# Four row blocks of the mixed activations split inside the sample's latent loop, and the rotary score products of two sequences issued as a pair

## The reference, cut to what matters

```
q = (rmsnorm(cq) @ w_q_up)                      # 8 MLA heads: 64 plain + 32 rotary columns each
s = (q_nope . k_nope + q_pe . k_pe) * MLA_SCALE # keys from the latent cache ckv, rotary keys kpe
o_mla = softmax(s) @ v
mixed = concat([o_mla (512), ret_y (256), o_sb (256)])
x = x + mixed @ w_out                           # 1024 x 1024
x = x + memory_attend(x); x = x + conv_ffn(x)
```

## Time and profile before

| | us |
|---|---|
| median of 3 runs | 1745.48 (1745.2 to 1748.55) |
| the profiled execution | 1748.12 |
| its span | 1746.3 |
| PE busy | 1703.1 (98%) |
| DVE busy | 1076.1 (62%) |
| ACT busy | 537.6 (31%) |
| POOL busy | 493.6 (28%) |
| granted clock of TensorE, mean | 0.996 |

### The profile page before, as it was taken

How to read it: one execution, slowest core, us unless ns; L and a number is a source line. 1 busy time by engine, 2 the same in 40 slices (tenths; PEclk the granted TensorE clock), 3 DMA queues, 4 the chain that set the end, 5 groups by cost and what they waited for, 6 DMA issues and landing times.

```text
span 1746.3 us, 26437 instructions
## 1 busy us (share of the span) xinstructions
PE 1703.1 (98%) x10471; PEld 1562.2 (89%) x10471; DVE 1076.1 (62%) x1439; ACT 537.6 (31%) x955; POOL 493.6 (28%) x219
## 2 busy tenths in 40 slices
PE   7999999999999989999999999999999999999997
PEld 7998899776666669998899999999999999999996
DVE  6864466786656644536487566565655656566567
ACT  6311121486655541114243220202112121121234
POOL 1772122000000103431044343333333424243331
PEclk9999999999999999999999999999999999999999
DMA  5222111411122303415311111111111111111113
GB/s 213 85 76 77 52 38 37 133 36 61 62 94 67 112 28 108 150 53 216 119 49 37 49 37 48 36 48 36 48 36 48 36 48 36 48 36 48 37 46 109
DMA packets 35005, 119.28 MB, mean 68 GB/s; under 512 B 4976, under 2 KB 8016, under 8 KB 32496
## 3 DMA queue, kind: packets, MB, share of 16 engines
q1 hardware_dynamic: 32624, 108.76, 19.2%
q10 hardware_dynamic: 2304, 9.44, 1.6%
HBM read 100.73 MB, written 15.17 MB: 66 GB/s over the span
## 4 chain that ended last, share of the span: by engine, by line
PE 93%; DVE 3%; ACT 2%; issue 1%; POOL 0%; DMA 0%; ACTq 0%; DVEq 0%; SPq 0%
PE scores L1931 35%; PE bank L1931 33%; PE scores L2159 3%; PE bank L2213 3%; PE bank L2237 2%; PE scores L2004 2%; PE bank L2263 2%; PE scores L1953 1%; PE scores L2179 1%; PE bank L1940 1%; PE scores L2337 1%; PE scores L2336 1%; DVE y_sumsq L1894 1%; PE bank L2230 1%; PE bank L2477 1%
## 5 line engine op out<-in xcount | busy, mean ns | idle before, releaser
L854 POOL TENSOR_TENSOR w_hi<-w_raw,zero 128x1024 fp32r<-128x1024 f32 x96 | 188.5, 1964 | 1179.9 <-PE bank L1931 477.6
L1931 PE MATMUL scores<-act_hi,w_hi 128*128 128x384 f32 x960 | 324.2, 338 | 0.0
L1931 PE MATMUL scores<-act_hi,w_lo 128*128 128x384 f32 x960 | 322.6, 336 | 0.0
L1931 PE MATMUL scores<-act_lo,w_hi 128*128 128x384 f32 x960 | 322.5, 336 | 0.0
L857 POOL TENSOR_TENSOR w_lo<-w_raw,w_hi 128x1024 fp32r<-128x1024 f32 x96 | 251.5, 2619 | 7.5
L1859 DVE TENSOR_TENSOR x<-bank,x 128x384 f32<-128x384 f32 x216 | 120.4, 558 | 103.6 <-PE bank L1931 103.6
L1931 PEld LDWEIGHTS scores<-act_hi,w_hi 128*128 128x128 f32 x960 | 180.5, 188 | 0.6 <-issue 0.2
L1931 PEld LDWEIGHTS scores<-act_lo,w_hi 128*128 128x128 f32 x960 | 180.5, 188 | 0.3 <-issue 0.2
L1931 PEld LDWEIGHTS scores<-act_hi,w_lo 128*128 128x128 f32 x960 | 180.5, 188 | 0.0
L1931 PE MATMUL bank<-act_hi,w_hi 128*128 128x384 f32 x528 | 177.9, 337 | 0.0
L1931 PE MATMUL bank<-act_hi,w_lo 128*128 128x384 f32 x528 | 177.4, 336 | 0.0
(11 more groups left out here) (348 smaller groups left out, 3164.9 us busy)
## 6 DMA issues: line engine op xcount, KB each, us to landing
w_raw<-wstream SPq DMA_DIRECT2D x108, 512.0 KB, 3.6
x_blk<-xT ACTq DMA_DIRECT2D x8, 576.0 KB, 4.7
x_mid<-x_blk ACTq DMA_DIRECT2D x8, 576.0 KB, 3.1
x<-x_mid SPq DMA_DIRECT2D x4, 1152.0 KB, 5.4
z<-cache_k SPq DMA_DIRECT2D x4, 1024.0 KB, 5.3
z<-cache_v SPq DMA_DIRECT2D x4, 1024.0 KB, 7.3
mk_c<-mk_c SPq DMA_DIRECT2D x4, 1024.0 KB, 12.6
mv_c<-mv_c SPq DMA_DIRECT2D x4, 1024.0 KB, 14.6
```

The source lines that it names most:

```text
L854: pool.tensor_tensor(w_hi[:, k], w_raw[:, k], zero[:].unsqueeze(2).to_broadcast([P, KB, P]), ALU.add).then_inc(w_rounded, 1)
L1931: mm = pe.matmul(out, w[:, k, at + kb], x(kb), start=first and kb == 0 and n == 0, stop=last and kb == n_kb - 1 and n == 2)
```

## The change

- The order becomes `MIX_ORDER = (5, 4, 6, 7, 0, 1, 2, 3)`. ACT rounds blocks 5, 4, 6, 7 after the values of sequences 0, 2, 4, 5; DVE splits them after its iterations 3, 5, 7, 8. Blocks 0 to 3 stay behind `o_heads`.
- `mix_hi` and `mix_lo` become one tile of 16 rows, with a row of its own for each block's high and low part (`MIX_HI`, `MIX_LO`), `o_lat` moves onto the first latent keys, `ckv_new` behind `w_v`.
- ACT rounds block 0 before it issues the two DMAs for `x_blk`, and the others after.
- PE: scores of sequences n and n+1 (n even) are started together. Iteration n waits for the exponential of n-1 and for the loads of both, does the latent products of n, then the rotary products of n and n+1 alternately (upper and lower half of the array, `S[0]` and `S[1]`); iteration n+1 does only the latent products of n+1.
- PE: row 0 and one chunk of row 1 are put after the loop's last scores, the rest of row 0 an iteration later, the rest of row 1 before `o_heads`, rows 2 and 3 directly after it.

```diff
-MIX_ORDER = (6, 7, 0, 1, 2, 3, 4, 5)
-
-MIX_AFTER = {4: 6, 6: 7}
+MIX_ORDER = (5, 4, 6, 7, 0, 1, 2, 3)
+N_MIX_EARLY = 4
+
+MIX_AFTER = {0: 5, 2: 4, 4: 6, 5: 7}
+SPLIT_AFTER = {3: 0, 5: 1, 7: 2, 8: 3}
+
+MIX_HI = (0, 1, 2, 3, 5, 8, 6, 7)
+MIX_LO = (10, 11, 12, 13, 4, 9, 14, 15)
...
             act.wait_ge(stored_kpe, 16)
+            round_mixed(MIX_ORDER[N_MIX_EARLY])
             for k in range(2):
                 act.dma_start(x_blk[:, k], io["xT"][:, k]).then_inc(xb_in[k], 16)
-            for kb in MIX_ORDER[2:]:
+            for kb in MIX_ORDER[N_MIX_EARLY + 1:]:
                 round_mixed(kb)
...
-                if n == DB - 2:
-                    split_mixed(0)
-
-            for i in range(1, KB):
+                if n in SPLIT_AFTER:
+                    split_mixed(SPLIT_AFTER[n])
+
+            for i in range(N_MIX_EARLY, KB):
                 split_mixed(i)
...
+            def mixed_row(i, chunks=range(NCH)):
+
+                pe.wait_ge(mix_split, i + 1)
+                projection_row(i, MIX_ORDER[i], mix, mix, chunks, MIX_HI, MIX_LO)
...
             for n in range(DB + 2):
                 if n < DB:
-                    pe.wait_ge(exp_done, N_ITEMS + n - 1)
-                    pe.wait_ge(lat_in[n], 64)
-                    rows = slice(64 * (1 - n % 2), 64 * (1 - n % 2) + 64)
-                    for at, w, latent, rotary in ((0, PAST, lat_k[n], lat_pe[n // 2][rows]),
-                                                  (PAST, TS, z[:, Z_CKV, TP:T], z[rows, Z_KPE, TP:T])):
-                        own_s = S[n % 2][:, at:at + w]
-                        pe.matmul(own_s, q_abs[:, n], latent, start=True, stop=False)
-                        mm = pe.matmul(own_s, q_pe[rows, n], rotary, start=False, stop=True)
+                    if n % 2 == 0:
+                        pe.wait_ge(exp_done, N_ITEMS + n)
+                        for b in (n, n + 1):
+                            pe.wait_ge(lat_in[b], 64)
+                    for at, w, latent in ((0, PAST, lat_k[n]), (PAST, TS, z[:, Z_CKV, TP:T])):
+                        mm = pe.matmul(S[n % 2][:, at:at + w], q_abs[:, n], latent, start=n % 2 == 0, stop=n % 2 == 1)
+                    if n % 2 == 0:
+                        for at, w in ((0, PAST), (PAST, TS)):
+                            for b in (n, n + 1):
+                                rows = latent_rows(b)
+                                rotary = lat_pe[n // 2][rows] if at == 0 else z[rows, Z_KPE, TP:T]
+                                rotated = pe.matmul(S[b % 2][:, at:at + w], q_pe[rows, b], rotary, start=b == n + 1,
+                                                    stop=b == n)
+                                if b == n:
+                                    mm = rotated
                     mm.then_inc(s_ready, 1)
                 if n == DB:
                     pe.wait_ge(w_split, W_OUT + 1)
-                    pe.wait_ge(mix_split, 1)
                     pe.wait_ge(exp_done, N_ITEMS + DB - 1)
-                    projection_row(0, MIX_ORDER[0], mix_hi, mix_lo, (0, 1))
+                    mixed_row(0, (0, 1))
+                    mixed_row(1, (0,))
...
                 if n == DB + 1:
-                    projection_row(0, MIX_ORDER[0], mix_hi, mix_lo, (2,))
+                    mixed_row(0, (2,))
...
-            pe.wait_ge(mix_split, 2)
-            projection_row(1, MIX_ORDER[1], mix_hi, mix_lo, (0, 1))
+            mixed_row(1, (1, 2))
             pe.wait_ge(o_evac, T_MLA_S + DB)
...
-            projection_row(1, MIX_ORDER[1], mix_hi, mix_lo, (2,))
             for i in range(2, KB):
-                pe.wait_ge(mix_split, i + 1)
-                projection_row(i, MIX_ORDER[i], mix_hi, mix_lo)
+                mixed_row(i)
```

More of the change, by code:

```diff
@@ L449, in build @@
         lat_v = [r(f"lat_v{b}", [P, PAST])[:] for b in range(2)]
-        ckv_new = r("ckv_new", [P, KVL])
         lat_v += [z[:, Z_SK + n // 2, PAST * (n % 2):PAST * (n % 2) + PAST] for n in range(6)]
@@ L455, in build @@
         w_v = r("w_v", [P, MH * VD])
-        o_lat = Region(at_pair[1], 4096)("o_lat", [P, DB, MH, DS])
+        ckv_new = r("ckv_new", [P, KVL])
+        o_lat = Region(at_pair[0], 4096)("o_lat", [P, DB, MH, DS])
         r = Region(off_b, NZ * ROW)
-        mix_hi = r("mix_hi", [P, KB, T], F32R)
-        mix_lo = r("mix_lo", [P, KB, T], F32R)
+        mix = r("mix", [P, 2 * KB, T], F32R)
         x_blk = r("x_blk", [P, 2, T])
@@ L1180, in round_mixed @@
             def round_mixed(kb):
-                act.activation(mix_hi[:, kb], mixed[:, kb], ACT.Copy).then_inc(mix_rounded, 1)
+                act.activation(mix[:, MIX_HI[kb]], mixed[:, kb], ACT.Copy).then_inc(mix_rounded, 1)
             for n in range(DB + 2):
@@ L1692, in split_mixed @@
                 kb = MIX_ORDER[i]
-                dve.tensor_tensor(mix_lo[:, kb], mixed[:, kb], mix_hi[:, kb].bitcast(F32),
+                dve.tensor_tensor(mix[:, MIX_LO[kb]], mixed[:, kb], mix[:, MIX_HI[kb]].bitcast(F32),
                                   ALU.subtract).then_inc(mix_split, 1)
@@ L1989, in _, with projection @@
             memory_sums()
-            def projection(k, slot, evacuated, hi, lo):
+            def projection(k, slot, evacuated, hi, lo, hi_row=range(KB), lo_row=range(KB)):
                 pe.wait_ge(w_split, slot + 1)
@@ L1995, in projection, with projection_row @@
                     pe.wait_ge(g_evac, evacuated + c + 1)
-                    mm = split_products(bank[3 * k + c][:, 0:CH], k, 0, KB, lambda kb: hi[:, kb, frames(c)],
-                                        lambda kb: lo[:, kb, frames(c)])
+                    mm = split_products(bank[3 * k + c][:, 0:CH], k, 0, KB, lambda kb: hi[:, hi_row[kb], frames(c)],
+                                        lambda kb: lo[:, lo_row[kb], frames(c)])
                     mm.then_inc(g_done if c < NCH - 1 else w_used, 1)
-            def projection_row(i, kb, hi, lo, chunks=range(NCH)):
+            def projection_row(i, kb, hi, lo, chunks=range(NCH), hi_row=range(KB), lo_row=range(KB)):
                 for c in chunks:
-                    for n, (w, x) in enumerate(((w_hi, hi), (w_hi, lo), (w_lo, hi))):
-                        mm = pe.matmul(bank[c][:, 0:CH], w[:, 0, kb], x[:, kb, frames(c)], start=i == 0 and n == 0,
+                    for n, (w, x, at) in enumerate(((w_hi, hi, hi_row[kb]), (w_hi, lo, lo_row[kb]), (w_lo, hi, hi_row[kb]))):
+                        mm = pe.matmul(bank[c][:, 0:CH], w[:, 0, kb], x[:, at, frames(c)], start=i == 0 and n == 0,
                                        stop=i == KB - 1 and n == 2)
@@ L2326, in _, with latent_rows @@
             pe.wait_ge(new_ready, 1)
+            def mixed_row(i, chunks=range(NCH)):
+                pe.wait_ge(mix_split, i + 1)
+                projection_row(i, MIX_ORDER[i], mix, mix, chunks, MIX_HI, MIX_LO)
+            def latent_rows(n):
+                return slice(64 * (1 - n % 2), 64 * (1 - n % 2) + 64)
             for n in range(DB + 2):
                 if n < DB:
-                    pe.wait_ge(exp_done, N_ITEMS + n - 1)
-                    pe.wait_ge(lat_in[n], 64)
-                    rows = slice(64 * (1 - n % 2), 64 * (1 - n % 2) + 64)
-                    for at, w, latent, rotary in ((0, PAST, lat_k[n], lat_pe[n // 2][rows]),
-                                                  (PAST, TS, z[:, Z_CKV, TP:T], z[rows, Z_KPE, TP:T])):
-                        own_s = S[n % 2][:, at:at + w]
-                        pe.matmul(own_s, q_abs[:, n], latent, start=True, stop=False)
-                        mm = pe.matmul(own_s, q_pe[rows, n], rotary, start=False, stop=True)
+                    if n % 2 == 0:
[13 more added lines that the diff above has]
+                                    mm = rotated
                     mm.then_inc(s_ready, 1)
@@ L2373, in _ @@
             mm.then_inc(o_heads, 1)
-            projection_row(1, MIX_ORDER[1], mix_hi, mix_lo, (2,))
             for i in range(2, KB):
-                pe.wait_ge(mix_split, i + 1)
-                projection_row(i, MIX_ORDER[i], mix_hi, mix_lo)
+                mixed_row(i)
             for m in range(1, KB):
-                projection(m % 2, W_OUT + m, 3 * (NZ + m - 2), mix_hi, mix_lo)
+                projection(m % 2, W_OUT + m, 3 * (NZ + m - 2), mix, mix, MIX_HI, MIX_LO)
             first_projection(W_MQ, G_MQ - 2 * NCH, x_split, KB, act_hi, act_lo)
```

## The result

The changed kernel takes 1737.3 us (median of 6 runs, 1734.3 to 1739.87), the one before 1745.47 (1745.2 to 1748.82). The ratio is 0.9947, with a 95% interval of 0.9931 to 0.9962: 8.2 us less between the medians, 9.3 by the ratio. The profiled execution took 1737.32, span 1735.5.

The account below looks back on a forecast made before the run. PE (98% busy) bounds the kernel through its work, waits and low clock. Gain 11.7 us (5.1 up to o_heads, 6.6 behind) less 1.3 for clock is 10.4: 1748.12 to 1737.7, median 1745.5 to 1735.1; range 1732.5 to 1741.

Parts of the forecast that it names:

- the offset to the median: Whole kernel: profiled execution taken as 2.6 us above the median of the runs, so 1737.7 gives a median of 1735.1.
- the drop of clock at the start: Loop's start, about 606 to 609: lower clock after two waits costs 1.3 us, bounds 0.8 and 3; no drop 0.15.
- What bounds it: PE, busy 98% of the span: never idle in the loop; behind it, 5.2 us of waits and about 7 at low clock.
- Eight rotary records 1.28: Loop, per pair of sequences: rotary products in alternate halves take 1.28 us instead of 2.94.
- the rival with the halves apart: Loop: halves don't run together, each pair costs 2.94 instead of 1.28, 6.6 us less gain, 1741.7; chance 0.07.
- Latent products 1.25 and 1.10: Loop: the two latent products take 1.25 us in even iterations, 1.10 in odd ones; bounds 1.08 and 1.28.
- The period: Loop, per pair: 7.7 us, set by the chain through DVE and ACT; PE's work 7.1, standing some 0.6.
- The waits at the start: Loop's start: PE waits 1.93 us before the first transposes and 1.55 before the second pair.
- The splits and roundings are hidden: Loop: four roundings (1.17 us) on ACT and four splits (1.37) on DVE hidden, the rounding by only 0.1.
- Behind the loop: After the loop: PE stands 0.2 us instead of some 5, clock stays up; first W_out block some 47.4 after loop's start.
- Nothing ahead of the loop moves: Ahead of the loop: no change counted there; the gain of 10.4 us was taken from the before execution's own 1748.12.

Follow-up runs that it names:

- e1: Kernel before with the paired scores alone; tiles, splits and projection rows as before; median 1745.15 us, ratio 0.999.
- e5: Changed kernel with the rotary operands of both sequences of a pair in the same half of the array; median 1740.5 us, ratio 0.9958.
- e7: Changed kernel with two of the four DVE splits moved behind even iterations (after 4, 5, 6, 8); median 1740.1 us, ratio 0.9959.
- e8: Changed kernel with the two DMA issues for x_blk ahead of the first rounding, as before; median 1738.08 us, ratio 0.9938.
- e3: Changed kernel with both rotary products of sequence n+1 issued first, then both of n; median 1737.15 us, ratio 0.9937.
- e9: Changed kernel with only two row blocks (5 and 4) rounded and split inside the loop; median 1742.67 us, ratio 0.9965.
- e6: Changed kernel with twelve extra products into an unread bank filling most of the two waits at the loop's start; median 1736.86 us, ratio 0.9948.
- the late wait: Changed kernel, but the even iteration waits for the exponential of n-1 only before its rotary products; median 1734.36 us, again 1734.41.

## Why the prediction was right

The time, 1737.3, is 2.2 above the value of 1735.1 and inside the range (1732.5 to 1741.0). The mechanism was right in the main: less work in the rotary products, PE never standing behind the head products, and a wait on DVE and ACT as the price. Two steps were off, though (the offset to the median and the drop of clock at the start), and two errors cancelled.

- *From the trace to the median.* The profiled execution of before was 2.6 above its median, and the text assumed the same of after (1737.7 and 1735.1). After's profiled execution lies 0.02 above its median. The traces differ by 12.0 us from the loop's start to the block's end; 1.15 of that is lost because after's loop started later, which gives the 10.8 between the two profiled executions, and the other 2.6 down to the 8.2 between the medians is this offset.
- *What the offset probably is.* With 59.09, 1087.2 and 1.8, the time of 1745.2 would need a loop that starts at 597.1, earlier than in any of 13 traces (598.35 at the least). With the clock up behind the head products, as in e1 (14.76 instead of 17.40), it needs 599.75, which is usual. So executions of before at 1745.3 most likely have no fall there, and the change then saves 9.4 us of the 12.0. No trace of such an execution exists, so this is an inference and not shown.
- *Two errors that cancelled.* For the profiled execution the forecast was 1737.7, and it took 1737.32. That it is so near is partly luck: the drop of clock at the loop's start, 1.3, didn't come in this execution, and its loop started 1.15 later than before's, which nobody had forecast.

Point by point:

- *What bounds it.* Right: PE's waits and low clock behind the loop, and PE work in the loop.
- *Eight rotary records 1.28.* Right in size. The mechanism was two things, not one: halves side by side 1.07, grouping 0.59 (e5). So the rival with the halves apart was priced too high, at 6.6: e5 lost some 3.9, since the grouping stays. An estimate by the span model of the Trainium skill (TensorE: Matmul & The Clock Gate, Part 3) would have had 1.47; the row decided rightly.
- *Latent products 1.25 and 1.10.* 1.28 (616.42 to the start of the rotary group, 617.70) and 1.10. The Trainium skill says that "Changing tiling mode (not just tile) drains the TensorE" (TensorEngine Tiling, Key Properties). The runs agree in direction: the same eight rotary records cost 2.94 in the old order, with eight changes between full and half height for two sequences, and 2.35 in one group in one half, with two (e5), 0.59 less.
- *The period.* 7.7 forecast, 7.69 measured, with DVE and ACT in the chain. PE's own work is a little longer than the text's 7.1 (5.54 from 616.42 to 621.96, then 0.60 and 1.12, so 7.26), and it stands for some 0.4 in each pair and not 0.6.
- *The waits at the start.* Forecast were the first transposes 5.56 behind the loop's start and the second pair 7.71 behind it; measured 5.58 (606.75) and 7.56 (608.73). The idle times in brackets, 1.67 and 1.21, are shorter than the forecast's 1.93 and 1.55, since they count from the end of the last record with its tail, and the second also since its pair starts 0.15 sooner.
- *The splits and roundings are hidden.* Right where they were put. In after's trace each exponential behind a rounding starts 0.31 us after ACT is free, so the cover on ACT was 0.3 and not 0.1. e1 and e7 show the cost of another place: 1.44 us for one split and 2.98 for two.
- *Behind the loop.* 47.4 forecast from start to block's end, 47.08 measured; 0.1 of waiting before the fifth row. The parts: 2.64 for the clock (17.40 against e1's 14.76; the text had 2.9), in an execution that has the fall, 0.92 for the issue order (e8), 3.1 for the rows that cover the chain (14.76 - 0.92 - 10.73).
- *The clock at the start.* This step failed for the trace shown: the text expected a drop after the two waits, at a cost of 1.3. Neither of the two traces of after has one, nor e1, e7 or e8. Three of the eight traces with both waits have it (e3, e5, e9), at 2.40, some 4.9 and 1.56. So "a drop in some executions, at 1.6 us or more" would have been right. The three traces with one or both waits filled or removed (e6 and two of the late wait) have none, but three are too few to tell that from chance.
- *Nothing ahead of the loop moves.* Also wrong as an assumption, though not by the change: the loop's start lies between 598.35 and 603.95.

Open: why the groups of times of before (mostly about 1745.3 and 1748.5) and of after (about 1734.4, 1737.3, 1739.9) are not filled alike, and how often the clock falls at 204 us, at 337 us and behind the head products in either kernel. The profiled executions are too few to say.

## What to carry to other kernels

A wait behind a chain of other engines costs twice if the clock falls after it: in e9's trace 3.3 us of standing brought 2.6 more, in e1's 3.5 us brought nothing more. So a gain read from one trace with such a fall in it can be larger than that of the median: look at several executions before you put the clock into the sum. Move work that is ready, however little (two row blocks of 1.55 us), to the exact place where the chain runs. When products are paired to save PE time, count what the pair now waits for: with PE faster, the chain through DVE and ACT set the period, places in the other engines' queues that had been free for a split were not free any more, and a wait put only before the product that needs it gave back 2.3 us.

Read a small change from fixed marks in the trace (start, head products, end of block); its stretches repeat within 0.1 us, while whole executions of one kernel differ by 5.6.

## What the runs showed of the hardware that was not expected

- Products in different row halves ran side by side even when the program issued two products of one half and then two of the other (e3: 1.29 us for eight records; in one half 2.35, e5). The records of the second half's 512 columns start beside the first's, ahead of the first's 128 columns in the program.
- The clock's falls differ from one execution to the next where the instructions are the same: at two waits of some 1.7 and 1.2 us with five transposes between them the lower level came in three traces of eight, from the transposes or from the second wait on, for 3.4, 6.8 and 10.2 us. Behind the head products it came in before and not in e1, after the same wait of 3.5 us.
- The cost of a fall differs with how long it lasts and how much work lies in it: 1.56, 2.40 and some 4.9 us at one and the same place.
